# Last stage of an encoder-layer kernel: one pass per tile against two passes over pairs of tiles with seven products

## What is computed

```python
merged = ga * (o_a' @ w_a) + gb * (o_b' @ w_b) + gc * (o_c' @ w_c)
x = x + merged @ w_out
x = x + sigmoid(rms_norm(x, ple_g) @ w_pg) * (p @ w_ple)
y = rms_norm(x, final_norm_g)          # rms_norm: x * rsqrt(mean(x^2) + eps) * g
```

## Time and profile before

| | us |
|---|---|
| median of 3 runs | 2713.71 (2712.07 to 2714.48) |
| profiled execution | 2716.89 |
| its span, first to last instruction | 2715.1 |
| PE busy | 2642.7, 97% of the span |
| DVE / ACT / POOL busy | 76% / 52% / 46% |
| mean granted clock of TensorE | 0.993 of 2.4 GHz |

### The profile page before, as it was taken

The page is one execution under the profiler, slowest core; times in us unless marked ns, Lnnn a source line. Parts: engine busy times, 40 slices in busy tenths (PEclk is TensorE's granted clock), DMA queues, the critical chain, the costliest instruction groups (busy, mean ns, idle before and its releaser), DMA issues. The chain is left out here.

```text
span 2715.1 us, 39945 instructions
## 1 busy us (share of the span) xinstructions
PE 2642.7 (97%) x13955; PEld 2455.2 (90%) x13955; DVE 2062.5 (76%) x4080; ACT 1404.5 (52%) x2406; POOL 1243.4 (46%) x850
## 2 busy tenths in 40 slices
PE   7999999999999999999999889999999999999998
PEld 7999999999999999999999767778789998888886
DVE  7377899999999999994543589999976557555555
ACT  5377578687877768755213477777720012111111
POOL 0100188686868686788345564322153342111110
PEclk9999999999999999999999999999999999999999
DMA  4433323243423232224565643221275555212211
GB/s 176 126 118 125 127 92 122 89 133 105 134 97 128 89 130 98 76 94 140 184 187 172 190 118 93 62 66 55 64 268 161 182 171 177 76 51 76 76 51 40
DMA packets 271575, 320.35 MB, mean 118 GB/s; under 512 B 36626, under 2 KB 234898, under 8 KB 270734
## 3 DMA queue, kind: packets, MB, share of 16 engines
q1 hardware_dynamic: 170691, 189.97, 22.9%
q10 hardware_dynamic: 100682, 127.82, 13.5%
HBM read 196.36 MB, written 120.73 MB: 117 GB/s over the span
## 5 line engine op out<-in xcount | busy, mean ns | idle before, releaser
L1737 PE MATMUL psum<-hT_hi,j_whi 128*128 128x416 f32 x2432 | 865.3, 356 | 3.9 <-DVE hT_lo L1812 2.5
L1737 PE MATMUL psum<-hT_hi,j_wlo 128*128 128x416 f32 x2432 | 853.2, 351 | 0.0
L1737 PE MATMUL psum<-hT_lo,j_whi 128*128 128x416 f32 x2432 | 851.9, 350 | 0.0
L1313 POOL TENSOR_TENSOR v_y<-v_y,v_product 128x422 f32<-128x422 f32 x459 | 557.8, 1257 | 84.9 <-ACT v_product L1295 84.9
L449 DVE TENSOR_SCALAR_CACHE_REDUCE s_tie<-s_key,s_bits 128x640 bf16<-128x640 f32 (+14 forms) x352 | 464.3, 1319 | 12.3
L1737 PEld LDWEIGHTS psum<-hT_hi,j_whi 128*128 128x128 f32 x2432 | 456.5, 188 | 14.0 <-issue 4.4
L1737 PEld LDWEIGHTS psum<-hT_lo,j_whi 128*128 128x128 f32 x2432 | 457.6, 188 | 9.1 <-issue 1.6
L1737 PEld LDWEIGHTS psum<-hT_hi,j_wlo 128*128 128x128 f32 x2432 | 456.4, 188 | 5.5
L1295 ACT ACTIVATE v_product<-v_x,v_taps 128x422 f32<-128x422 f32 x510 | 304.3, 642 | 103.9 <-POOL v_y L1313 81.7
L1577 ACT ACTIVATE j_out<-psum 128x416 f32<-128x416 f32 x285 | 144.6, 508 | 305.8 <-PE psum L1737 291.5
L1516 POOL TENSOR_TENSOR j_wlo<-j_w,j_whi 128x1024 fp32r<-128x1024 f32 x59 | 145.0, 2457 | 313.6 <-ACT j_whi L1557 313.6
(11 more groups left out here) (329 smaller groups left out, 4891.1 us busy)
## 6 DMA issues: line engine op xcount, KB each, us to landing
T_dram<-j_out ACTq DMA_DIRECT2D x58, 624.0 KB, 2.9
j_w<-in_w_in ACTq DMA_DIRECT2D x59, 512.0 KB, 3.9
T_dram<-j_out ACTq DMA_DIRECT2D x60, 416.0 KB, 2.4
m_gate<-T_dram SPq DMA_DIRECT2D x60, 416.0 KB, 3.4
m_oraw<-B_dram SPq DMA_DIRECT2D x15, 832.0 KB, 5.3
M_dram<-m_merged ACTq DMA_DIRECT2D x5, 1664.0 KB, 7.5
n_x<-in_x_prompt SPq DMA_DIRECT2D x16, 512.0 KB, 6.1
f_mraw<-M_dram SPq DMA_DIRECT2D x16, 512.0 KB, 4.7
```

Of the source, the lines that this page charges most:

```text
L1313: pool.tensor_tensor(y[k % 2][:], y[k % 2][:], product[n % RING][:], ALU.add).then_inc(added, 1)
L1737: last = pe.matmul(bank, w[p][:, k, :], h[:, k, t0:t0 + SPAN], start=(k == 0 and q == 0), stop=(k == KD - 1 and q == 2))
```

## The change

The last stage goes in two passes over 8 pairs of tiles, with the sample apart. In the first pass `x + merged @ w_out` is made and stored to a new `X_dram`; in the second it is transposed, multiplied by the gate's weights and finished. The last two pairs of the first pass stay in SBUF and come first in the second. Each 256 x 1024 by 1024 x 1024 product of a pair is cut in 2 x 2 blocks (the two tiles by two halves of the depth, and halves of the columns) and made by Strassen's scheme in Winograd's form: seven products of 128 x 512 by 512 x 512, each 12 matmuls, with sums of blocks ahead on the input (`sums`, `fourth_sum` on POOL) and behind on the output (on DVE, from PSUM). The sums of weight blocks are made once, on POOL in `stage_merge`, and go through a new `G_dram`; the norm's `ple_g` is multiplied into the gate weights there (ACT, `W_dram`), and the root `rstd` is no longer multiplied to `x`: ACT's sigmoid takes it as its scale. The sample takes four products of 12 matmuls per pass. POOL now makes all low parts of the pairs and the last addition to `x`; ACT makes all high parts. In `stage_trunk` one `low` goes ahead of `root`.

```diff
@@ stage_trunk: vector
         for b, tiles in enumerate(GROUPS[1:], 1):
             following = GROUPS[b + 1] if b + 1 < len(GROUPS) else range(0)
+            low(tiles[0])
             if following:
                 root(following)
-            for t in tiles:
+            for t in tiles[1:]:
                 low(t)
@@ stage_merge
+    LOW_WEIGHTS_AT = ((LAST - 1, 3), (LAST - 1, 6), (LAST, 1), (LAST, 3), (LAST, 5))
@@ stage_merge: gpsimd
             split_input(c, pool, s)
+            if 0 <= s - 2 < SUMS:
+                c.sums_of_weights(pool, s - 2)
+            if s == SUMS + 3:
+                c.first_sums(pool)
@@ stage_merge: scalar
+        c.load_gain(act)
+        for z in range(2):
+            c.load_rows(act, z)
         for span in range(len(SPANS)):
+            for z in ((0, 1), (2, 3, 4), (5, 6, 7), (), ())[span]:
+                c.store_sums(act, z)
+                if z + 2 < SUMS:
+                    c.load_rows(act, z + 2)
+                if 4 <= z + 1 < SUMS:
+                    c.scale_rows(act, z + 1)
...
@@ stage_merge: vector
+                if (s, n) in LOW_WEIGHTS_AT:
+                    c.low_of_weight(vec, LOW_WEIGHTS_AT.index((s, n)))
@@ stage_finish
+FIRST_PASS = [0, 1, 2, 3, 4, 5, None, 6, 7]
+SECOND_PASS = [6, 7, 0, 1, 2, 3, 4, 5, None]
+A11_B11, S2_T2, S3_T3, S1_T1, A22_T4, S4_B22, A12_B21 = range(PRODUCTS)
...
+    def sums(pool, n):
+        if n < PAIRS:
+            pool.wait_ge(m_full, 16 * (n + 1))
+        else:
+            pool.wait_ge(raw_done, 2 * (n - PAIRS) + 2)
+        if n:
+            pool.wait_ge(lo_done, PRODUCTS * n)
+        pool.tensor_tensor(s1[:], a21, a22, ALU.add).then_inc(sum_done, 1)
+        pool.wait_ge(sum_done, 4 * n + 1)
+        pool.tensor_tensor(s2[:], s1[:], a11, ALU.subtract).then_inc(sum_done, 1)
+        pool.tensor_tensor(a21, a11, a21, ALU.subtract).then_inc(sum_done, 1)
+
+    def low(pool, n, j):
+        pool.wait_ge(hi_done, PRODUCTS * n + j + 1)
+        pool.tensor_tensor(a_lo[j][:], SOURCE[j], f32(a_hi[j][:]), ALU.subtract).then_inc(lo_done, 1)
...
+        def load_merged(n):
+            pair = [p for p in FIRST_PASS if p is not None][n]
+            sp.wait_ge(lo_done, PRODUCTS * n)
+            sp.dma_start(a_raw[:], c.M_dram[:, :, 2 * P * pair:2 * P * (pair + 1)].rearrange("s q t -> q s t")).then_inc(m_full, 16)
...
+        sums_stored(sp)
+        load_x(0)
         c.merged_stored(sp)
+        sp.dma_start(s_raw[:], c.M_dram[:, :, SEQ:TOK].rearrange("s q t -> q s t")).then_inc(s_full, 16)
+        load_x(1)
+        load_merged(1)
...
@@ stage_finish: tensor
+        def ple(q, h):
...
+            if h == H21:
+                pe.wait_ge(mult_done, nth(q, H22))
...
+        for q in range(PAIRS):
+            for j in range(PRODUCTS):
+                product(9 + q, PAIRS + q, j)
+                if j == S2_T2:
+                    turn_p(q)
+                elif j == S3_T3:
+                    turn(q + 1, 0)
+                elif j == S1_T1 and q:
+                    ple(q, H22)
+                elif j == A22_T4 and q + 1 < PAIRS:
+                    turn(q + 1, 1)
+                elif j == S4_B22 and q:
+                    for h in (H21, H12, H11):
+                        ple(q, h)
...
@@ stage_finish: scalar
+        for q in range(PAIRS):
+            n = PAIRS + q
+            if q:
+                sigmoid(q - 1, H11)
+            high(act, n, A12_B21)
+            if q:
+                last_squares(q - 1)
...
+            copy_first(9 + q, n)
...
+            high_of_p(q)
...
+                copy_turned(q + 1, 0)
+                high(act, n + 1, A11_B11)
...
+            sigmoid(q, H22)
...
+                copy_turned(q + 1, 1)
+            sigmoid(q, H21)
+            if q + 1 < PAIRS:
+                for j in (S2_T2, S3_T3, S1_T1):
+                    high(act, n + 1, j)
...
```

More of the change, by code:

```diff
@@ L2776, in stage_finish @@
[L2776 to L2787 removed]
+    a_raw = sb("f_araw", [P, KD, 2 * P])
@@ new lines, in stage_finish @@
+    pT = bank(BANK_P).rearrange("q (b k n) -> q b k n", b=2, k=KP)
+    HALVES = ((1, 1, c22, BANK_P), (1, 0, u3, BANK_P), (0, 1, u2, BANK_T), (0, 0, p1s, BANK_T + 1))
+    cols = lambda n: slice(n * HALF_D, (n + 1) * HALF_D)
+    tile_of = lambda x, t: x[:, t, :]
+    x_half = lambda x, t, n: x[:, t, cols(n)]
+    two_tiles = lambda rows, pair: rows[2 * P * pair:2 * P * (pair + 1), :].rearrange("(b t) d -> t b d", t=P)
+    uses_of = lambda x, first, second: sum(y is x for y in x_of_first[:first]) + sum(
+        y is x and q > 1 for q, y in enumerate(x_of_second[:second]))
@@ new lines, in low, with first_sums, first_highs @@
+    def low(pool, n, j):
+        pool.wait_ge(hi_done, PRODUCTS * n + j + 1)
+        pool.tensor_tensor(a_lo[j][:], SOURCE[j], f32(a_hi[j][:]), ALU.subtract).then_inc(lo_done, 1)
+    def first_sums(pool):
+        sums(pool, 0)
+        low(pool, 0, A11_B11)
+    def first_highs(act):
+        for v in range(2):
+            high_of_weight(act, v)
+        for v in range(3, 5):
+            load_weight(act, v)
+        for v in range(2, 4):
+            high_of_weight(act, v)
+        for j in range(1, 3):
+            high(act, 0, j)
+        high_of_weight(act, 4)
+        load_weight(act, 5)
+        load_weight(act, 6)
+        high(act, 0, S1_T1)
@@ new lines, in ple @@
+        def ple(q, h):
+            t, half, _, b = HALVES[h]
+            rows = P if SECOND_PASS[q] is not None else DEC
+            pe.wait_ge(p_lo_done, q + 1)
+            if q == 0:
+                pe.wait_ge(w_lo_done, 2 * PRODUCTS + 1)
+            if h == H21:
+                pe.wait_ge(mult_done, nth(q, H22))
+            elif h == H12:
+                if q < 7:
+                    pe.wait_ge(raw_done, 2 * q + 4)
+                elif q == 7:
+                    pe.wait_ge(s_lo_done, 2)
+                else:
+                    pe.wait_ge(mult_done, nth(q - 1, H12))
+            elif h == H11 and q == 8:
+                pe.wait_ge(mult_done, nth(q - 1, H11))
+            for k in range(KP):
+                for x, (left, right) in enumerate(((p_hi, wp_hi), (p_lo, wp_hi), (p_hi, wp_lo))):
+                    last = pe.matmul(bank(b)[0:rows, :], left[:, t, k, 0:rows], right[:, k, cols(half)], start=(k == 0 and x == 0),
+                                     stop=(k == KP - 1 and x == 2))
+            last.then_inc(ple_done, 1)
@@ new lines, in sample @@
+        def sample(i, m, between):
+            rows = slice(0, DEC)
+            a = s_hi, s_lo
+            w = lambda j: (w_hi[j], w_lo[j])
+            first, second, third = (bank(b)[rows, :] for b in (BANK_A, BANK_B, BANK_D))
+            n = 6 if m == 0 else 2 * PAIRS
+            pe.wait_ge(s_lo_done, m + 1)
+            pe.wait_ge(p1s_done, i)
+            three(first, a, w(A11_B11), range(KH)).then_inc(s_product, 1)
+            between(0)
+            pe.wait_ge(c_done, nth_c(n - 1, H21))
+            three(second, a, w(S1_T1), range(KH), stop=False)
+            three(second, a, w(S4_B22), range(KH, KD), start=False).then_inc(s_product, 1)
+            between(1)
+            pe.wait_ge(c_done, nth_c(n - 1, H12))
+            three(third, a, w(A12_B21), range(KH, KD)).then_inc(s_product, 1)
@@ new lines, in end @@
+        def end(q):
+            if q == 0:
+                vec.wait_ge(fing_full, 16)
+            for t in (1, 0):
+                x = tile_of(x_of_second[q], t)
+                vec.scalar_tensor_tensor(out=x, in0=x, scalar=rstd[:, 2 + t:3 + t], in1=fin_g[:], op0=ALU.mult, op1=ALU.mult
+                                         ).then_inc(finished, 1)
+        for v in range(5, PRODUCTS):
+            low_of_weight(vec, v)
+        n = 0
+        for e, pair in enumerate(FIRST_PASS):
+            if pair is None:
+                first_pass_of_sample(e)
+                continue
+            first_pass(e, n, e == 8)
+            n += 1
@@ new lines, in vector @@
+        c11(PAIRS - 1)
+        multiply(PAIRS - 1, H11)
+        low_of_p(8)
+        sum_of_sample(17, 1)
+        roots(8)
+        end(PAIRS - 1)
+        rows, x = slice(0, DEC), x_of_second[8]
+        for h, buf in ((H12, u2), (H11, p1s)):
+            _, half, _, b = HALVES[h]
+            part = x[rows, 0, cols(half)]
+            if h == H11:
+                vec.wait_ge(s_product, 6)
+                vec.tensor_tensor(p1s[rows], p1s[rows], bank(BANK_D)[rows, :], ALU.add).then_inc(c_done, 1)
+            vec.wait_ge(sig_done, nth(8, h))
+            vec.wait_ge(ple_done, nth(8, h))
+            vec.tensor_tensor(buf[rows], buf[rows], bank(b)[rows, :], ALU.mult).then_inc(mult_done, 1)
+            vec.wait_ge(mult_done, nth(8, h))
+            vec.tensor_tensor(part, part, buf[rows], ALU.add).then_inc(x_added, 1)
```

935 lines of the change are left out of this document (633 added, 302 removed).

## The result

The changed kernel takes **2686.49 us** (median of 4 runs, 2684.92 to 2691.63); the kernel before took 2714.1 us beside it (4 runs, 2712.07 to 2715.78). The ratio is 0.9902, interval 0.9885 to 0.9919: 27.6 us faster, where 12.2 were forecast. Direction and range hold, the size is more than twice the forecast. The profiled execution took 2691.63 us (span 2689.5, clock 0.991), 5.1 over its median.

A forecast was written before the change was run, and what follows sets the result against it. PE was taken to bound the kernel. Last stage 180.9 + 32 + 172.2 + 27.5 + 25.7 = 438.3 against 450.9; with +1.0 -0.6, 12.2 less: 2704.7 profiled, median 3.18 under, 2701.5 us; range 2680 to 2725.

The forecast's parts named there:

- a stall of 2 us ahead of H21 in each pair: Second pass, steady pairs: PE's `w_ple` product of H21 waits for DVE's multiplication of H22; period 28.7 us, not 26.7.
- The forecast's own formula: Second pass, period T of a steady pair: T = 26.7 + (50.6 - T - 19.9), giving 28.7 us.
- the mechanism: First pass: load and POOL's chain follow one another through the single buffer, 21.5 us a pair over PE's 19.1.
- the 1.1 for collisions: First pass: POOL charged 1.1 us per pair, between 0.2 and 2.8, for four DVE sums of SBUF tiles.
- the Trainium skill's rule: DVE and POOL on SBUF: whichever starts second waits in full; first-pass sums cost POOL up to 2.8 us per pair.
- The second pair's start: First pass: the load stands on SP behind other transfers, so the second pair starts at 25.0 us (22 to 28).
- The POOL rival: Both passes: POOL at 1.51 us per instruction sets the pace, 2723 us; gain gone from 1.41; chance 0.20.
- The clock's: Last stage: matmuls run at the lower clock behind stalls; free in first pass, 0.8 x 7 in loop: 2707; chance 0.10.
- With half of the waits hidden, 2685: Last stage: half of PE's waits hidden, 2685 us; chance 0.15 together with the case of PE staying the bound.
- PE's bound: Last stage: PE stays the bound, loads hidden, no stall at H21; stage 405 us, kernel 2668; chance 0.15 with half-hidden waits.
- The other two signs of being wrong: PE's idle in the last stage under 10 us in all, or `stage_merge` more than 5 us longer.
- the 1.0 charged there: `stage_merge`: the span's store may land later and delay DVE's gating; 1 us charged, from 0 to 10.

The follow-up runs named there:

- Experiment 7: Changed kernel with the second pass's addition of H11 moved from POOL to DVE and ACT's copy of the first product ahead of the squares: 2682.71 us.
- experiment 1: Changed kernel with DVE's two scalings of `end` moved behind the multiplication of H22 in the second pass: 2688.45 us.
- experiment 3: Changed kernel with the first pass's transposed pairs going by turns to two buffers instead of one: 2682.81 us.
- experiment 4: Changed kernel with DVE's two low weight halves at the last stage's start moved behind POOL's seventh low part of the first pair: 2688.7 us.
- experiment 9: Changed kernel with DVE's low half of the first gate-weight block moved behind its first addition in the first pass's last pair: 2685.0 us.

## Why the prediction was right, and where it failed

- **PE bounds the stage, and a matmul taken away is worth 0.227 us.** Right: 19.04 per pair of the first pass, 26.76 per pair of the second where nothing is waited for (19.1 and 26.7 forecast).
- **The step that failed: "a stall of 2 us ahead of H21 in each pair".** The loop exists and passes over the engines that were named; it was mis-sized. From a pair's start to the end of H22's multiplication it is 47.3 us, not 50.6. POOL loses 0.85 to `end`, not 1.9, and DVE loses nothing to POOL there, where 1.2 were charged: 2.2 of the 3.3 are this one collision, charged to both sides. POOL's pace was right (13 instructions in 16.6 without that loss); the other 1.0 is in DVE's steps, of a few tenths each. The forecast's own formula then gives a period of (26.76 + 47.3 - 19.9) / 2 = 27.1, and 27.17 was measured. By that formula half of an error reaches the pair: 3.3 us were 1.5 per steady pair, 7.3 over five; the second pair, which waits for other things, was 0.4 over its 28.7; together 6.9, half of what the sum was over (14.1). Experiment 7 shows the loops as the cause: the chain cut short left PE's 26.76. The half itself is worked out and not tested, for experiment 1 came to lengthen the second loop, not this one.
- **First pass: the mechanism was right (experiment 3), its price for four pairs 3.4 us too high.** A turn of the buffer takes 20.3 to 21.2, not 21.5. The load took 6.4, not 5.9, but of the 1.1 for collisions nothing was paid in two turns and 0.45 in two: most of DVE's sums of SBUF tiles fall where POOL waits for the load. By the Trainium skill's rule that was set beside it (page "SBUF — State Buffer", section "SBUF: two separate sides") the sum would have been 7 us longer; the rule holds where the two do meet (last section), but here they seldom met.
- **The second pair's start: the right time for the wrong reason.** 25.0 forecast, 24.0 measured; but the load was not behind SP's queue, it had not been issued: POOL's low parts, slowed by two weight halves on DVE that I had costed at nothing, held it to 13.0 us. The two halves also ended 11.9 us after the first matmul, not at 10, and PE waited 1.5 us for DVE's first sum behind them. With these out of the way the transfers that I had named do hold it (experiment 4).
- **First pair of the second pass, last pair, end.** 32, 27.5 and 25.7 against 30.8, 26.3 and 24.9. DVE's list is what holds the first (experiment 9).
- **The rivals.** The POOL rival is out, though the mean of its instruction in the last stage came to 1.41 us, the limit that was set: 177 of the 200 took 1.29 on the mean, and the time is in 23 that met DVE (last section), not in all of them. The clock's came once: 6.0 us at the lower level behind the gap of 2.98, 3.0 lost in time in which PE would have waited anyway, as the rival had it for the first pass; behind the first pass's later gaps of 1.2 and 1.8 the matmuls kept their pace, and in the second pass nothing was lost. "With half of the waits hidden, 2685" is the figure that came out (of the 33 us that the sum stood over PE's bound of 405, 19 were measured), and it had too little of the 0.15 given to PE's bound. The other two signs of being wrong stayed away: PE's idle in the stage is 13 us, not under 10, and `stage_merge` is no longer than before.
- **Merge and trunk.** The merge's transfers did slow down (the span's store lands in 11.4 us, before 7.5), and PE waited for none of them: between 1700 and 2264 us its waits are the same three as before. From the merge's first matmul to the last stage's it is 273.6 us in both kernels (272.1 to 274.4 in the variants), so nothing of the 1.0 charged there is seen. In the trunk the wait of 0.58 is gone and that of 2.45 stayed (2.52): from the `hT_hi` matmul ahead of them to the one behind it is 14.6 us in the changed kernel and all its variants and 15.3 before, so the moved `low` gave 0.7, where 0.6 were forecast; it was not tried alone. That the last stage's first matmul came 1.1 us later, against 0.4 forecast, lies within the spread of 12.8 us told above. Another 2 us of the miss are the median's: it stands 5.1 under the profiled execution, where 3.2 were carried over.

## What to carry over

Where engines run in a ring, add up the ring's length against the bound engine's own period, and ask of each collision which side started first: charging both sides turned a tie into a stall. A buffer that is loaded again only when its last reader is done adds load and chain; double it before making either faster. When a wait goes away, look for the next limit just behind it (a queue, the same lock, another ring): here two lay within a few us of one another in three places, and a move that only reordered a full engine's list brought nothing, while one that used an earlier gap of it did.
